# Bias and norm rows on 4 partitions, the bias table two chunks later, and the left-over quarter's first products behind two whole chunks, in a two-layer diffusion step with experts

## What is computed

```python
for l in range(2):
    mod = silu(cvec) @ w_ada[l] + b_ada[l]              # 1024 x 6144, six vectors: shift, scale, gate, twice
    h = rms_norm(x, norm_g[l, 0]) * (1 + sc_m) + sh_m
    p = h @ w_in[l]                                     # 1024 x 2816: q, k, v, u, v_mlp, B, C, h
    # 8 heads of attention: context tokens among themselves;
    # latent tokens over a 2-D window, with a bias from rpb[l] and a mask, and over the cached context
    y = concat(attention, u * (w_s @ norm(v_mlp) + b_s), B * conv3(C * h)) @ w_out[l]
    x = x + gt_m * rms_norm(y, norm_g[l, 1])
    h = rms_norm(x, norm_g[l, 2]) * (1 + sc_f) + sh_f
    if l == 0: f = (silu(h @ w_g) * (h @ w_u)) @ w_d    # 1024 x 2816 twice, 2816 x 1024
    else:      f = sum over the 2 chosen of 8 experts of gate * the same with the expert's weights
    x = x + gt_f * rms_norm(f, norm_g[l, 3])
```

## Time and profile before

| | |
|---|---|
| median of 3 runs | 1600.64 us |
| profiled execution, its own time | 1607.02 us |
| its span, first to last instruction | 1605.2 us |
| mean granted TensorE clock | 0.987 |
| busy: TensorE, VectorE, ScalarE, GpSimd | 1526.6, 1016.7, 865.0, 169.3 us |
| bytes over DMA | 429.33 MB, mean 267 GB/s |
| head and layer 0's input projection, to some 207 us | loads at 300 to 400 GB/s up to 60 us, later in bursts |
| dense feed-forward of layer 0 | some 245 to 545 us |
| experts | from some 750 us; 93.6 us for one of 1 tile |
| the two experts with a quarter | end at some 1445 and 1578 us |

### The profile page before, as it was taken

The page is one execution under the profiler, slowest core; times in us unless marked ns, Lnnn a source line. Parts: engine busy times, 40 slices in busy tenths (PEclk is TensorE's granted clock), DMA queues, the critical chain, the costliest instruction groups (busy, mean ns, idle before and its releaser), DMA issues.

```text
span 1605.2 us, 26359 instructions
## 1 busy us (share of the span) xinstructions
PE 1526.6 (95%) x11100; PEld 1240.8 (77%) x11100; DVE 1016.7 (63%) x935; ACT 865.0 (54%) x874; POOL 169.3 (11%) x175
## 2 busy tenths in 40 slices
PE   3989999999999999998999999999999989999993
PEld 3767777888888788787888888888888878777872
DVE  1425664333323554567988889888888966765665
ACT  1525543232222554546777777777777755554553
POOL 3120000000000310013002030300303010002001
PEclk8999999999999999999999999999999999999997
DMA  9994254777666573145999999999999988778882
GB/s 304 332 276 149 83 156 132 226 221 250 214 213 261 144 250 117 56 152 205 380 367 384 379 375 387 369 381 374 384 374 379 388 299 274 265 266 283 273 284 95
DMA packets 216658, 429.33 MB, mean 267 GB/s; under 512 B 23346, under 2 KB 64370, under 8 KB 215904
## 3 DMA queue, kind: packets, MB, share of 16 engines
q1 hardware_dynamic: 200448, 397.99, 71.1%
q0 software_dynamic: 14272, 22.66, 4.9%
q10 hardware_dynamic: 1808, 6.86, 1.1%
HBM read 422.65 MB, written 22.45 MB: 277 GB/s over the span
## 4 chain that ended last, share of the span: by engine, by line
PE 88%; DVE 4%; DMA 3%; ACT 2%; issue 1%; SPq 1%; ACTq 0%; POOL 0%; DVEq 0%; POOLq 0%
PE ps L1584 26%; PE ps L1586 25%; PE ps L1585 25%; PE ps L2087 3%; PE ps L1626 2%; DMA raw<-in_w_in_dram 2%; PE ps L2120 1%; PE ps L2054 1%; DMA raw<-in_w_ada_dram 1%; ACT whi L747 1%; DVE wlo L1078 1%; PE ps L1772 1%; DVE x L1176 1%; PE ps L1756 1%; PE ps L1741 1%
## 5 line engine op out<-in xcount | busy, mean ns | idle before, releaser
L1078 DVE TENSOR_TENSOR wlo<-raw,whi 128x2048 fp32r<-128x2048 f32 x327 | 745.8, 2290 | 343.0 <-ACT whi L747 249.7
L747 ACT ACTIVATE whi<-raw 128x2048 fp32r<-128x2048 f32 x327 | 626.4, 1918 | 470.1 <-PE ps L1586 233.0
L1584 PE MATMUL ps<-whi,xhi 128*128 128x512 f32 (+1 forms) x1352 | 536.6, 397 | 5.2 <-DVE xlo L1156 3.4
L1586 PE MATMUL ps<-whi,xlo 128*128 128x512 f32 (+1 forms) x1352 | 523.3, 387 | 0.0
L1585 PE MATMUL ps<-wlo,xhi 128*128 128x512 f32 (+1 forms) x1352 | 523.1, 387 | 0.0
L1584 PEld LDWEIGHTS ps<-whi,xhi 128*128 128x128 f32 x1352 | 255.0, 189 | 63.6 <-issue 9.7
L1586 PEld LDWEIGHTS ps<-whi,xlo 128*128 128x128 f32 x1352 | 254.8, 188 | 52.9
L1585 PEld LDWEIGHTS ps<-wlo,xhi 128*128 128x128 f32 x1352 | 255.2, 189 | 47.2
L1584 PE MATMUL ps<-whi,hhi 128*128 128x512 f32 x484 | 192.8, 398 | 0.0
L1586 PE MATMUL ps<-whi,hlo 128*128 128x512 f32 x484 | 188.9, 390 | 0.0
L1585 PE MATMUL ps<-wlo,hhi 128*128 128x512 f32 x484 | 188.6, 390 | 0.0
(11 more groups left out here) (231 smaller groups left out, 1054.6 us busy)
## 6 DMA issues: line engine op xcount, KB each, us to landing
raw<-in_w_moe_gu_dram SPq DMA_DIRECT2D x352, 512.0 KB, 5.7
raw<-in_w_moe_d_dram SPq DMA_DIRECT2D x176, 512.0 KB, 5.1
raw<-in_w_ada_dram SPq DMA_DIRECT2D x96, 512.0 KB, 6.2
raw<-in_w_in_dram SPq DMA_DIRECT2D x44, 512.0 KB, 5.2
raw<-in_w_ffn_gu_dram SPq DMA_DIRECT2D x44, 512.0 KB, 7.2
raw<-in_w_ffn_d_dram SPq DMA_DIRECT2D x22, 512.0 KB, 6.3
raw<-in_w_out_dram SPq DMA_DIRECT2D x16, 512.0 KB, 4.2
bias<-rpb_rows POOLq DMA_DIRECT2D x32, 96.0 KB, 6.4
```

The lines of the kernel that those rows point to most:

```text
L747: act.activation(whi[m % SPL][:, :], raw[n % RING][:, :], ACT.Copy).then_inc(s_hi, 1)
L1078: dve.tensor_tensor(wlo[n % RING][:, :], raw[n % RING][:, :], whi[NTH[n] % SPL][:, :].bitcast(F32), ALU.subtract).then_inc(s_lo, 1)
L1584: pe.matmul(out, a_hi, w_hi, start=start, stop=False)
L1586: return pe.matmul(out, a_lo, w_hi, start=False, stop=stop)
```

## The change

Bias and norm rows go to partitions g, g + 32, g + 64, g + 96 for g = 0 and 1 by two small DMAs; both buffers are zeroed first, ahead of the first bias rows. Layer 0's table is issued behind `WIN_SEQ[5]`, ("win", 0, 3), and its mask moves to just before `soft` of unit 4. In an expert with a quarter TensorE takes chunk 0, turns the rows, takes chunk 1, and then the small products of chunks 0 to 3; chunk 0 is counted as finished after its small products. ScalarE waits for those of chunks 2 and 3 before its first gate of the quarter.

```diff
             def brow(l, i):
...
-                pool.dma_start(brow_of[:, i % 2, :],
-                               bass.AP(b_ada.tensor, b_ada[l, 512 * i:512 * i + 512].offset, [[P, 4], [0, 32], [1, P]])
-                               ).then_inc(s_brow[i % 2], 16)
+                for g in range(2):
+                    pool.dma_start(brow_of[g:P:32, i % 2, :],
+                                   b_ada[l, 512 * i:512 * i + 512].rearrange("(j n) -> j n", j=4)
+                                   ).then_inc(s_brow[i % 2], 16)
             def norm_row(l, j):
...
-                for h in range(2):
-                    pool.dma_start(grow[:, h, :], bass.AP(norm_g.tensor, norm_g[l, j, 512 * h:512 * h + 512].offset,
-                                                          [[P, 4], [0, 32], [1, P]])).then_inc(s_gb, 16)
-
+                for g in range(2):
+                    pool.dma_start(grow[g:P:32, :, :], norm_g[l, j].rearrange("(h j n) -> j h n", h=2, j=4)
+                                   ).then_inc(s_gb, 16)
+
+            chain(pool.memset(brow_of[:, :, :], 0.0))
+            chain(pool.memset(grow[:, :, :], 0.0))
             brow(0, 0)
             brow(0, 1)
...
-                    pool.wait_ge(s_pe, PLACE["win", 0, WIN_SEQ[3]] + 1)
+                    pool.wait_ge(s_pe, PLACE["win", 0, WIN_SEQ[5]] + 1)
                     bias_rows(l)
...
                     if quarter:
                         w = rest_width(b)
+                        if b == 0:
+                            act.wait_ge(s_rest, N_REST * e + 2)
...
-                dve.wait_ge(s_brow[i % 2], 16 * (ADA_B // 2 * l + i // 2 + 1))
+                dve.wait_ge(s_brow[i % 2], 32 * (ADA_B // 2 * l + i // 2 + 1))
...
                         for u in units_at(j, 0):
+                            if u == N_OWN and l == 0:
+                                masked_bias(l)
                             if u == N_OWN:
                                 dve.wait_ge(s_bias, l + 1)
                             soft(l, u)
...
-                    if p == (3 if l else 6):
+                    if p == 3 and l:
                         masked_bias(l)
...
-                more(T, quarter, e)
+                if not quarter:
+                    more(T, quarter, e)
                 for c in range(N_GU):
                     ins = gate_up_chunk(c)
                     if quarter and c == 0:
-                        rest_split(0)
+                        more(T, quarter, e)
+                        continue
+                    if quarter and c == 1:
+                        pe_done(rest_split(0))
                         ins = rest_split(1)
                     pe_done(ins)
-                    if quarter and c % 2 == 0:
+                    if quarter and c == 1:
+                        rest(2)
+                        rest(3)
+                    if quarter and c and c % 2 == 0:
                         rest(c + 2)
                         rest(c + 3)
```

## The result

The changed kernel took **1592.67 us** (median of 5, 1591.75 to 1593.87) beside 1600.64 us for the kernel before on the same chip: ratio 0.9949, 95% interval 0.9937 to 0.9961, a gain of 8.0 us. The forecast was 1590.1 with a range of 1586.5 to 1596.3, so the time lies inside it, 2.6 us above the forecast. The profiled execution of the changed kernel took 1592.39 us around a span of 1590.7; that of before took 1607.02 around a span of 1605.2, 6.4 us above its own median. So the two spans differ by 14.5 us where the runs differ by 8.0. What follows is therefore read beside a second profile of the kernel before as well.

A forecast was written before the change was run, and what follows sets the result against it. TensorE was taken to bound the kernel, with time to gain only where it idles or runs at half clock. Rows 1.2, table less mask 7.4 and experts 1.9 sum to 10.5 us: 1590.1 us, range 1586.5 to 1596.3.

The forecast's parts named there:

- What bounds the kernel: Whole kernel: TensorE carries 88% of the chain, so time comes only where it stands still or runs at half clock.
- The hole: Layer 0's input projection: TensorE idles 7.26 us before turns of q, held by the late load of ("win", 0, 4).
- Together 9.2 us: Layer 0's input projection, table issued later: 6.9 us of idle TensorE go and 2.3 us come back from full clock.
- 1.8 us are lost: Layer 0's first softmaxes: the moved mask puts unit 5's scores 14.0 us after the first instead of 12.2.
- The collision: Rival: the table delays ("win", 0, 8) instead, 6 us more holding up ScalarE; gain 4.5, 1596.1 us; chance 0.08.
- I take 1.2: Head: bias and norm rows as small DMAs bring the first projection weights 1.2 us earlier; bounds 0 and 2.3.
- 1.9 us for both: Two experts with a left-over quarter: TensorE's new order gains 1.1 us in the first and 0.8 in the second.
- 2.4 us are lost inside it, released by 'issue': Run of 192 small products in the second quarter expert: took 7.9 us against 5.5 counted, with no semaphore explaining it.
- the case that the lost time stays: Rival: issue gaps remain in both quarter experts, which then give -2.1 us; 1594.1 us; chance 0.25.
- the same work in it, so the same saving: Whole kernel: the runs' median, 6.4 us under the profiled execution, was taken to gain the same 10.5 us.
- The slower one: Rival: the table lands 15.9 us late for its mask, before unit 4's softmax; 1606.0 us; chance 0.04.
- the marks set: Signs: full clock near 113 us, mask near 139 to 141, 1.4 us idle at chunk 2, issue gaps about 1 us.

The follow-up runs named there:

- different rows: Kernel before with each bias row read from 128 different rows of w_ada instead of four pieces of b_ada read 32 times: 1597.58 us, ratio 0.9977.
- the expert part alone: Kernel before with only TensorE's new order in experts with a left-over quarter and ScalarE's wait: 1604.27 us, ratio 1.0029.
- rows alone: Kernel before with only the bias and norm rows on 4 partitions, the two memsets and their semaphore count: 1596.02 us, ratio 0.9974.

## Why the prediction was near, and which steps failed

The sum was 1.2 + 7.4 + 1.9 = 10.5; the runs gave 8.0. It came close in part by luck: the rows brought 3 us more than their term and the experts some 4 to 7 less.

**What bounds the kernel: held.** The hole, its releaser and its size stand in every profile without the table's move, 6.8 to 7.4 us, and in none with it.

**"Together 9.2 us": held.** The load of ("win", 0, 4) took 5.1 us where I had 5.9; the first scores moved 14.3 us against the first profile of before, 4.6 of which are the head's: 9.7, and 8.9 to 9.1 against the second. The landing of the table, forecast for 135.4 to 136.3 on the clock of before, or 25.8 to 26.7 us behind the turns of q, is seen where a mask waited for it: 133.17 - 105.82 = 27.4 us in one kernel and 134.09 - 104.84 = 29.3 in the other. In the change the mask starts 30.5 us behind the turns of q with no wait, so the margin is 1.3 to 3.2 us where I had put 4. The collision did not move to ("win", 0, 8).

**"1.8 us are lost" to the mask: the size held, a consequence was missed.** 13.96 - 12.24 = 1.7, just as worked out from layer 1's pattern. But the wait of 2.40 us is idle time of TensorE, and I had costed it as idle time only. In five of seven profiles the clock fell behind it, for 1.5 us more in four and 2.9 in one. I had used that very effect to count 2.3 us behind the hole.

**"I take 1.2" for the rows: mis-sized.** It measured 4.2 us by the runs, outside the bounds of 0 and 2.3. The rate of the table's 256-byte pieces, 204 GB/s, was taken as the worst price of small pieces; these rows are larger pieces, but each is read 32 times. (Eight such transfers are issued before 43.26 us and not seven, the last at 42.57, too late to weigh.) The Trainium skill (DMA: Bandwidth & Descriptors, section "Specifications") gives 512 bytes as the least transfer for full rate. If these pieces of 512 bytes went at the full 351 GB/s of the loads, my estimate by that rule is 1.3 us. The runs show 4.2 for these transfers, so the measurement decides: pieces of that size do not by themselves bring the full rate. With different rows the runs leave 0.5 us, the first split of the profile some 2 to 3.

**"1.9 us for both" experts: the step that failed outright.** It rested on "2.4 us are lost inside it, released by 'issue'", and on chunk 1 hiding them. I had given the case that the lost time stays (0.25), but not the case that there is none: those gaps stood in one execution, which was 6.4 us slower than the median, and in none of the other eight profiles of that order. The lost time was measured rightly, 3.3 and 2.4 us, but it was nearly all of that execution's excess. I had written that the median had "the same work in it, so the same saving". Without the gaps there is nothing to hide, and only the added wait is left: forecast 1.4 us, measured 1.70 in each expert, less 0.16 for xsum. What the first expert loses beyond that (135.76 or 134.97 for 132.9, so 2.1 to 2.9 in all) was not forecast. Behind the branch TensorE's first work is now chunk 0, which needs VectorE's split, where it was turns that waited for no semaphore. In the repeated profile TensorE starts as that split ends; in the first one and in the expert part alone it starts 0.8 and 0.7 us after, so that part is not VectorE's wait and stays open.

**The gaps themselves.** What they were was not found; they never came back. In the profiles of the old order TensorE's first instruction behind the branch stood 1.4 to 2.3 us with no semaphore to wait for, and no other instruction of the two experts did, but in the first profile of before. Apart from that profile, this agrees with the Trainium skill (Runtime: NRT & Kernel Launch, section "Instruction fetch mechanics"), by which fetch is mostly hidden but behind a taken branch; that it is fetch no run here shows.

**The rivals.** The slower one (table too late for its mask) did not come, but its mechanism is real: with the mask at its old place a wait of 5.85 us for the table stood as 5.85 us on TensorE. Of the marks set, "issue" gaps of about 1 us in the runs did not show; the idle at chunk 2 and full clock at 113 us did. The projection weights came 4.3 us earlier and not one (rows alone), and the mask, forecast for 139 to 141, at 135.57, since the head had gained more.

**A better version.** Rows and table without the expert part: 1588.03 and 1590.18 us, 0.992 and 0.993 of the kernel before. With the mask ahead of the split it is as fast, and its wait is 1.3 us shorter. A version in which the plain products of chunk 2 stand ahead of the split ones would free VectorE earlier; in this form they share a PSUM bank with sums in progress, and it wasn't tried.

## What to carry to other kernels

Before a gap without a semaphore is costed, see it in a second profile; the profiled execution's distance from the median says whether to doubt it (here 6.4 us, of which 5.9 were lost around such gaps). When a transfer is moved, move its consumer as well, and price the consumer's new place by who waits behind it: 1.7 us for a net gain of 6 here. Small products that read raw weights should have a full chunk between them and the chunk that they hold up; without it each place here idled TensorE for 1.70 us.

## What the runs showed of the hardware that was not expected

- Transfers of 64 KB that read four pieces of 512 bytes 32 times each slow what runs beside them by far more than their bytes: those of the head cost some 4 us. With distinct source rows of the same size, in fewer packets, the runs were 3.7 us shorter. While the old transfers were under way the DMA engines stood at the same busy share (1.04) and moved 373 and 341 GB/s where they moved 405 and 389 without them.
- The same idle time of TensorE, 2.40 us at the same instruction, was followed by 1.2 GHz in five profiles and by 2.4 GHz in two; a wait of 1.11 us there by full clock in the one profile that had it. Behind the branch, too, idle times of 1.58, 1.65, 2.06 and 2.32 us were followed by the lower clock, and others of 1.41 to 2.05 us, in six profiles, were not.
- Profiles of one kernel differ by up to 6 us in their spans, and the differences sit in few places: the head (up to 2.4 us between two profiles of the change's kind), the first instruction behind a branch (up to 0.9), the clock behind it (1.7), and single runs of small products with gaps (5.9 in two experts).
